# Token factors of the first block's residuals and norms: computed on columns, spread by TensorE between modulation slots

## Chip, core and metric

The kernel runs on one core of a Trainium2 chip. The metric is the device time of one execution in microseconds; lower is better. All arithmetic of the stages told of here is in 32-bit floats.

## What is computed

Two transformer blocks run one after the other on 256 tokens of width 1024. The first block (two layers) carries 256 context tokens along; its residual stream X therefore has 512 tokens until the middle of the second layer. Every norm in it has a gain and a shift that come from a small conditioning network (a vector times a 1024 x 6144 matrix for each layer):

```
rmsnorm(x, g) = x * rsqrt(mean(x*x) + EPS) * g
modulate(x, shift, scale) = x * (1 + scale) + shift
```

A layer does this twice, once with a mixer and once with a feed-forward part f:

```
y = f(modulate(rmsnorm(x, g0), shift, scale))
x = x + gate * rmsnorm(y, g1)
```

So each half of a layer has a norm in front of f and a residual behind it, and both need one factor for each token: 1 / sqrt(mean square + EPS).

## The kernel before

All activations lie with features on partitions: X is eight chunks of 128 features, each 128 partitions x n tokens (n is 512 or 256). The sum over features is therefore a sum over partitions, and TensorE makes it with a stationary matrix of ones: the result, wk[:, 0, 0:n], holds each token's sum on all 128 partitions at once. ScalarE takes the root of 128 x n values, VectorE the reciprocal of 128 x n values, and the factor multiplies each chunk.

The pieces, by their line numbers in the profile:

- A residual r (0 to 3): ScalarE squares each chunk of the branch's output Y as it arrives (L975), GpSimd adds them up in sq_acc (L982, L985). pe_residual makes one matmul for the sum (L990); act_residual takes the root (L995), with a table load ahead of it; dve_residual the reciprocal (L1001), and then for each chunk nt = Y times the factor (L1013) and X += gain times nt (L1007).
- A norm j (1 to 3): ScalarE squares each updated chunk of X (L743), pe_norm accumulates the sum chunk by chunk (L730), then root (L747) and reciprocal (L765), nt = X times the factor (L777), scaled and shifted by ScalarE (L757, "n" in the profile), rounded to the high part (L760), and the low part on VectorE (L772). The next projection takes high and low parts chunk by chunk.
- Residual 0 is followed by norm 1, residual 1 by norm 2 (both pairs on 512 tokens), residual 2 by norm 3 (256 tokens), residual 3 (256 tokens) by the second block's first norm, which the diff doesn't touch. Norm 0 isn't touched either.
- The conditioning matrices are worked off in modulation slots of 1 MB, spread over the first block wherever TensorE has room. A slot is eight matmuls (16 passes) of 256 columns in a quarter of the array each (L570, pe_ada_products), a staging copy by ScalarE (L580), and four passes with two moving columns that turn the previous slot's result onto partitions (L593, pe_ada_columns). Its weights lie in a ring of two buffers (ada_ring). ScalarE asks for the load of slot s + 2 only when it has staged slot s (L583).

The engines' programs are written out by hand, and each runs in its own order. In the pair residual 0 and norm 1, TensorE has nine slots (0 to 8 of the stage): 0 and 1, the residual's matmul, 2 and 3, then the norm's chunks with slots 4, 5, 6 behind chunks 1, 3 and 5, then 7 and 8. ScalarE stages 0 and 1, takes the root, stages 2 and 3, squares the norm's chunks with 4, 5 and 6 staged behind chunks 3, 5 and 7, takes the root, stages 7 and 8 (the `meanwhile` of act_norm), and only then scales. The pair residual 1 and norm 2 has the same order. A 32-bit matmul is two passes in the profile, each with its own weight load.

Of the kernel before, what the change touches and what calls it, by code (L numbers as in the profile page):

```python
# [20 lines left out]
ALU = mybir.AluOpType  # L21
# [3 lines left out]
P = 128  # L25
D = 1024
# [145 lines left out]
def stack_kernel(nc, t, out, layers):  # L172
# [3 lines left out]
    with ctx:  # L176
# [45 lines left out]
        sq = at("sq", [P, 2, T1], nt0 + 2 * KB)  # L222
        root = at("root", [P, T1], nt0 + 6 * KB)
        rstd = at("rstd", [P, T1], nt0 + 8 * KB)
        nt = at("nt", [P, 2, T1], nt0 + 10 * KB)
        n32 = at("n32", [P, 2, T1], nt0 + 14 * KB)

# [265 lines left out]
        def V(name, i=0, n=1):  # L493
            return vec[:, VEC[name] + i:VEC[name] + i + n]
# [228 lines left out]
        def squares_of(j):  # L723
            return (sq4, None, root4) if j == 4 else (sq2, sq2_acc, root2)

        def pe_norm(pe, j, between=None):
            n = NORMS[j][0]
            for c in range(DC):
                pe.wait_ge(nsq_ready, DC * j + c + 1)
                pe.matmul(wk[:, 0, 0:n], ones[:, :], sq[:, c % 2, 0:n], start=c == 0, stop=c == DC - 1)\  # L730
                    .then_inc(nsq_used, 1)
                if between:
                    between(c)

        def act_norm(act, j, meanwhile=None, between=None):
            n, x0, groups, gain, shift = NORMS[j]
            if j == 0:
                act.wait_ge(s_vec, 16)
            for c in range(DC):
                x_ready_for(act, j, c)  # L740
                if c >= 2:
                    act.wait_ge(nsq_used, DC * j + c - 1)
                act.activation(sq[:, c % 2, 0:n], X[:, c, x0:x0 + n], ACT.Square).then_inc(nsq_ready, 1)  # L743
                if between:
                    between(c)
            act.wait_ge(nsq_used, DC * (j + 1))
            act.activation(root[:, 0:n], wk[:, 0, 0:n], ACT.Sqrt, bias=V("eps"), scale=1.0 / D).then_inc(root_ready, 1)  # L747
            if meanwhile:
                meanwhile()
            act.wait_ge(s_gain, (4, 6, 8, 9)[j])  # L750
            for c in range(DC):
                act.wait_ge(nt_ready, DC * j + c + 1)
                if c >= 2:
                    act.wait_ge(h_ready, DC * j + c - 1)
                for i, (s, a, b) in enumerate(groups):
                    kw = {} if shift is None else {"bias": shift(s, c)}
                    ins = act.activation(n32[:, c % 2, a:b], nt[:, c % 2, a:b], ACT.Identity, scale=gain(s, c), **kw)  # L757
                ins.then_inc(n32_ready, 1)
                act.wait_ge(n32_ready, DC * j + c + 1)
                act.activation(H_hi[n][:, c, 0:n], n32[:, c % 2, 0:n], ACT.Copy).then_inc(hhi_ready, 1)  # L760

        def dve_norm(dve, j, meanwhile=None):
            n, x0, groups, gain, shift = NORMS[j]
            dve.wait_ge(root_ready, j + 1)
            dve.reciprocal(rstd[:, 0:n], root[:, 0:n]).then_inc(rstd_ready, 1)  # L765
            if meanwhile:
                meanwhile()
            dve.wait_ge(rstd_ready, j + 1)

            def lo(c):  # L770
                dve.wait_ge(hhi_ready, DC * j + c + 1)
                dve.tensor_tensor(H_lo[n][:, c, 0:n], n32[:, c % 2, 0:n], H_hi[n][:, c, 0:n].bitcast(F32),  # L772
                                  ALU.subtract).then_inc(h_ready, 1)
            for c in range(DC):
                if c >= 2:
                    dve.wait_ge(n32_ready, DC * j + c - 1)
                dve.tensor_tensor(nt[:, c % 2, 0:n], X[:, c, x0:x0 + n], rstd[:, 0:n], ALU.mult).then_inc(nt_ready, 1)  # L777
                if c >= 1:
                    lo(c - 1)
            lo(DC - 1)  # L780
# [56 lines left out]

        def dve_rstd(dve, j):
            n = WIDTH[j]
            dve.wait_ge(root_ready, j + 1)  # L840
            dve.reciprocal(rstd2[:, 0:n], squares_of(j)[2][:, 0:n]).then_inc(rstd_ready, 1)
            dve.wait_ge(rstd_ready, j + 1)

        BY_POOL = (3, 7)

        def final_norm(eng, by_pool):
            eng.wait_ge(rstd_ready, FINAL + 1)
# [90 lines left out]
        yroot_ready, yrstd_ready, yt_ready = sem("y_root_ready"), sem("y_rstd_ready"), sem("y_scaled_ready")  # L938

        def dve_y(dve, name, add=None, tail=None):  # L940

# [42 lines left out]
                    pool.wait_ge(ysq_used, DC * r + m)  # L984
                    pool.tensor_tensor(sq_acc[:, 0:n], sq_acc[:, 0:n], sq[:, m % 2, 0:n], ALU.add).then_inc(ysq_used, 1)  # L985

        def pe_residual(pe, r):
            n = RES[r][0]
            pe.wait_ge(ysq_used, DC * (r + 1))
            pe.matmul(wk[:, 1, 0:n], ones[:, :], sq_acc[:, 0:n], start=True, stop=True).then_inc(ysum_ready, 1)  # L990

        def act_residual(act, r):
            n = RES[r][0]
            act.wait_ge(ysum_ready, r + 1)
            act.activation(root[:, 0:n], wk[:, 1, 0:n], ACT.Sqrt, bias=V("eps"), scale=1.0 / D).then_inc(yroot_ready, 1)  # L995

        def dve_residual(dve, r):
            n, x0, groups, (layer, j), _ = RES[r]
            dve.wait_ge(s_gain, (5, 7, 8, 9)[r])
            dve.wait_ge(yroot_ready, r + 1)  # L1000
            dve.reciprocal(rstd[:, 0:n], root[:, 0:n]).then_inc(yrstd_ready, 1)  # L1001
            dve.wait_ge(yrstd_ready, r + 1)

            def update(c):
                dve.wait_ge(yt_ready, DC * r + c + 1)
                for s, a, b in groups:
                    ins = dve.scalar_tensor_tensor(X[:, c, x0 + a:x0 + b], nt[:, c % 2, a:b], gains[:, layer, j, s, c:c + 1],  # L1007
                                                   X[:, c, x0 + a:x0 + b], ALU.mult, ALU.add)
                ins.then_inc(x_ready, 1)
            for c in range(DC):  # L1010
                if c >= 2:
                    dve.wait_ge(x_ready, DC * r + c - 1)
                dve.tensor_tensor(nt[:, c % 2, 0:n], Y[:, c, 0:n], rstd[:, 0:n], ALU.mult).then_inc(yt_ready, 1)  # L1013
# [1719 lines left out]
        def pe_ffn_halves(pe, layer, j):  # L2733
            def slots(s):
                if ADA_FFN + s < ADA_LATE:
                    pe_ada(pe, ADA_FFN + s)
                elif ADA_FFN + s == ADA_LATE:
                    pe_ada_close(pe, ADA_LATE)
            pe_ffn(pe, layer, 0, j, slots if layer == 0 else None)
            pe_ffn(pe, layer, 1, j)  # L2740
            if layer == 0:
                for g in (0, 1):
                    pe_ada(pe, ADA_LATE + g)
            pe_residual(pe, j)
            if layer == 0:
                for g in (2, 3):
                    pe_ada(pe, ADA_LATE + g)

# [133 lines left out]
        def _(pe):  # L2882
# [14 lines left out]
                    ks=(0, 1, 2, 4, 5, 6, 7, 3), fill=lambda s, j: pe_hyb_out(pe, s, j))  # L2897
            for g in (0, 1):
                pe_ada(pe, ADA_OUT + g)
            pe_residual(pe, 0)  # L2900
            for g in (2, 3):
                pe_ada(pe, ADA_OUT + g)
            pe_norm(pe, 1, between=lambda c: pe_ada(pe, ADA_OUT + 4 + c // 2) if c in (1, 3, 5) else None)
            for g in (7, 8):
                pe_ada(pe, ADA_OUT + g)
            pe_ffn_halves(pe, 0, 1)
            pe_norm(pe, 2, between=lambda c: pe_ada(pe, ADA_LATE + 4 + c // 2) if c in (1, 3, 5) else None)
            for g in (7, 8):
                pe_ada(pe, ADA_LATE + g)
# [176 lines left out]
```

## Time and profile before

| what | us |
|---|---|
| median of 3 runs | 2080.07 |
| lowest and highest run | 2079.8, 2082.15 |
| profiled execution, its own time | 2080.6 |
| its span in the trace | 2078.9 |
| TensorE busy in the span | 1969.3 |
| VectorE busy | 1249.3 |
| ScalarE busy | 939.3 |

The span runs from the first to the last instruction; the profiled execution's own time is 1.7 us longer. TensorE's clock has two levels, 2.4 GHz (shown as 1.00) and 1.2 GHz (0.50); over the whole span the mean granted clock is 0.977.

### The profile page before, as it was taken

To read this page: it belongs to the slowest core of one execution; us is meant where nothing else is said; L and a number is where in the kernel's file an instruction comes from. 1 tells how busy PE (TensorE), PEld (TensorE's weight loads), DVE (VectorE), ACT (ScalarE), POOL (GpSimd) and SP (SyncE) were. 2 spreads that over 40 slices of the span, in tenths; PEclk is the share of its full clock that TensorE was granted. 3 is DMA by queue.
4 is the path that set the end of the run, shared out by engine and by line. 5 is a ranking of instruction groups with operands and counts; after the bars stand their busy time and mean duration, and the time that the engine had idled before them with its cause. 6 is when DMAs were issued, how large, how long until landed. Compare 5 with 4: busy or idle time off the path is not lost.

```text
span 2078.9 us, 33997 instructions
## 1 busy us (share of the span) xinstructions
PE 1969.3 (95%) x13365; PEld 1745.7 (84%) x13365; DVE 1249.3 (60%) x1809; ACT 939.3 (45%) x1464; POOL 288.3 (14%) x245
## 2 busy tenths in 40 slices
PE   5999989999999899999979998999999999989998
PEld 3776747778888489989969997998899999879997
DVE  6355355543654545667567676656975566787564
ACT  4344445322332332258466455346654444565353
POOL 2000113430542000021024140000010010000001
PEclk9999989999999899999989999999999999989999
DMA  8621464433223523222434544542344544324553
GB/s 356 214 78 61 162 223 154 171 115 118 83 87 104 182 101 123 82 81 82 145 126 157 186 162 138 183 149 82 134 159 173 181 166 143 110 87 168 183 182 122
DMA packets 43950, 296.77 MB, mean 143 GB/s; under 512 B 4976, under 2 KB 6128, under 8 KB 11696
## 3 DMA queue, kind: packets, MB, share of 16 engines
q1 hardware_dynamic: 36576, 247.48, 34.5%
q10 hardware_dynamic: 6048, 42.49, 5.9%
q0 software_dynamic: 1200, 5.02, 0.6%
q8 instruction: 91, 1.49, 0.3%
q14 instruction: 35, 0.29, 0.0%
HBM read 293.93 MB, written 1.05 MB: 142 GB/s over the span
## 4 chain that ended last, share of the span: by engine, by line
PE 83%; DVE 7%; ACT 4%; DMA 2%; issue 2%; POOL 1%; SPq 0%; ACTq 0%; DVEq 0%; POOLq 0%
PE acc L456 23%; PE acc L458 22%; PE acc L457 22%; DVE w_lo L393 2%; PE acc L451 2%; PE wk L570 2%; PE acc L452 2%; PE acc L453 2%; PE wk L1599 1%; DMA ada_first<-in_w_ada 1%; PE wk L730 1%; ACT w_hi L383 1%; PE wk L593 1%; DMA ada_ring<-in_w_ada 1%; PE wk L1329 1%
## 5 line engine op out<-in xcount | busy, mean ns | idle before, releaser
L456 PE MATMUL acc<-Hhi,w_hi 128*128 128x272 f32 (+2 forms) x2304 | 745.5, 324 | 31.1 <-DVE Hlo L772 9.1
L458 PE MATMUL acc<-Hhi,w_lo 128*128 128x272 f32 (+2 forms) x2304 | 721.9, 313 | 0.0
L457 PE MATMUL acc<-Hlo,w_hi 128*128 128x272 f32 (+2 forms) x2304 | 721.2, 313 | 0.0
L393 DVE TENSOR_TENSOR w_lo<-w_raw,w_hi 128x1024 fp32r<-128x1024 f32 (+2 forms) x472 | 586.8, 1282 | 201.1 <-ACT w_hi L383 199.5
L383 ACT ACTIVATE w_hi<-w_raw 128x1024 fp32r<-128x1024 f32 (+2 forms) x472 | 452.6, 1005 | 436.0 <-PE acc L458 356.7
L456 PEld LDWEIGHTS acc<-Hhi,w_hi 128*128 128x128 f32 x2304 | 441.9, 192 | 77.1 <-issue 36.6
L457 PEld LDWEIGHTS acc<-Hlo,w_hi 128*128 128x128 f32 x2304 | 442.3, 192 | 21.7
L458 PEld LDWEIGHTS acc<-Hhi,w_lo 128*128 128x128 f32 x2304 | 441.7, 192 | 22.5
L456 PE MATMUL acc<-Fhi,w_hi 128*128 128x256 f32 (+2 forms) x864 | 264.7, 306 | 5.1 <-POOL Flo L1086 5.1
L458 PE MATMUL acc<-Fhi,w_lo 128*128 128x256 f32 (+2 forms) x864 | 264.4, 306 | 0.0
L457 PE MATMUL acc<-Flo,w_hi 128*128 128x256 f32 (+2 forms) x864 | 264.1, 306 | 0.0
L456 PEld LDWEIGHTS acc<-Fhi,w_hi 128*128 128x128 f32 x864 | 163.4, 189 | 13.5 <-POOL Flo L1086 6.4
L458 PEld LDWEIGHTS acc<-Fhi,w_lo 128*128 128x128 f32 x864 | 163.5, 189 | 7.0
L457 PEld LDWEIGHTS acc<-Flo,w_hi 128*128 128x128 f32 x864 | 163.1, 189 | 6.6
L1042 ACT ACTIVATE cgu<-acc,vec 128x512 f32<-128x512 f32 (+1 forms) x88 | 58.2, 667 | 149.7 <-PE acc L458 149.5
L1064 DVE SCALAR_TENSOR_TENSOR cgu<-acc,vec,cgu 128x510 f32<-128x510 f32 (+1 forms) x88 | 52.1, 609 | 96.9 <-ACT cgu L1042 96.9
L451 PE MATMUL acc<-w_hi,Hhi 128*128 128x256 f32 x320 | 93.2, 291 | 0.0
L1083 POOL TENSOR_TENSOR hid<-sg,cgu 128x512 f32<-128x512 f32 (+1 forms) x44 | 44.8, 1018 | 335.4 <-ACT sg L1046 335.4
L452 PE MATMUL acc<-w_lo,Hhi 128*128 128x256 f32 x320 | 90.4, 283 | 0.0
L453 PE MATMUL acc<-w_hi,Hlo 128*128 128x256 f32 x320 | 90.4, 283 | 0.0
L813 POOL TENSOR_TENSOR sq_acc<-sq 128x272 f32<-128x272 f32 (+1 forms) x4 | 4.8, 1204 | 526.2 <-ACT sq L796 376.6
L1086 POOL TENSOR_TENSOR Flo<-hid,Fhi 128x256 f32 (+3 forms) x44 | 71.9, 1635 | 7.4 <-POOL Fhi L1084 7.0
(381 smaller groups left out, 2432.8 us busy)
## 6 DMA issues: line engine op xcount, KB each, us to landing
w_raw<-in_w_ffn_in SPq DMA_DIRECT2D x44, 1024.0 KB, 4.9
ada_ring<-in_w_ada ACTq DMA_DIRECT2D x40, 1024.0 KB, 4.9
w_raw<-in_w_mlp_in SPq DMA_DIRECT2D x32, 1024.0 KB, 4.8
w_raw<-in_w_mlp_out SPq DMA_DIRECT2D x32, 1024.0 KB, 4.9
w_raw<-in_w_ffn_out SPq DMA_DIRECT2D x32, 704.0 KB, 4.0
ada_first<-in_w_ada SPq DMA_DIRECT2D x8, 1024.0 KB, 18.1
w_raw<-in_w_ret_v SPq DMA_DIRECT2D x8, 1024.0 KB, 4.7
w_raw<-in_w_ret_g SPq DMA_DIRECT2D x8, 1024.0 KB, 4.8
```

Of the source, the lines that this page charges most:

```text
L383: act.activation(w_hi[:, r, a:b], w_raw[:, r, a:b], ACT.Copy).then_inc(hi_done, 1)
L393: dve.tensor_tensor(w_lo[:, r, a:b], w_raw[:, r, a:b], w_hi[:, r, a:b].bitcast(F32), ALU.subtract).then_inc(lo_done, 1)
L451: pe.matmul(o, x_hi(k)[:, toks], w_hi[:, r, w], start=k == 0, stop=False)
L452: pe.matmul(o, x_hi(k)[:, toks], w_lo[:, r, w], start=False, stop=False)
L453: mm = pe.matmul(o, x_lo(k)[:, toks], w_hi[:, r, w], start=False, stop=k == last)
L456: pe.matmul(o, w_hi[:, r, w], x_hi(k), start=k == 0, stop=False)
L457: pe.matmul(o, w_hi[:, r, w], x_lo(k), start=False, stop=False)
L458: mm = pe.matmul(o, w_lo[:, r, w], x_hi(k), start=False, stop=k == last)
L1042: act.activation(cgu[:, r, c, 0:n], acc_tile(p, r, c), ACT.Identity, bias=Vd("conv_b", m + layer * 44), scale=Vd("conv_w", m + (layer * 3 ...
L1064: dve.scalar_tensor_tensor(seqs(o, 1, SEQ), seqs(acc_tile(p, r, c), 0, SEQ - 1), w, seqs(o, 1, SEQ), ALU.mult, ALU.add).then_inc(conv_left, 1)
L1083: pool.tensor_tensor(hid[:, r, 0:n], left(r), right(r), ALU.mult).then_inc(hid_mul, 1)
L1086: pool.tensor_tensor(lo, hid[:, r, 0:n], hi.bitcast(F32), ALU.subtract).then_inc(hid_done, 1)
```

## The change

In the four residuals and in norms 1, 2 and 3 the square sums are made with tokens on partitions: for each tile of 128 tokens the squares are the stationary operand and one column of ones moves, so that the result is one column of 128 sums. Root and reciprocal then work on 128 x n/128 values (rcol). To bring the factor back to all partitions, VectorE scales the identity by it, one 128 x 128 diagonal for each tile, and TensorE multiplies ones by that diagonal (dve_spread, pe_spread); the factor is then read from PSUM (wk) by the scaling. pe_norm puts its sums into acc instead of wk.

TensorE's order changes: slot 2 now lies between a residual's sum and its spread, slot 3 behind the spread; in norms 1 and 2 slot 7 moves into the chunk loop, behind chunk 7, then comes the spread, then slot 8. ScalarE's order of slots stays. Semaphores of residuals and norms are merged (nth, spread_base).

The diff without its one-line renumberings of waits:

```diff
+        diag, rcol = root, at("rcol", [P, 8], nt0 + 8 * KB)
...
+        def pe_spread(pe, j, residual):
+            n, base = NORMS[j][0] if not residual else RES[j - 1][0], spread_base(j, residual)
+            for t in range(n // P):
+                pe.wait_ge(s_diag, base + t + 1)
+                pe.matmul(wk[:, 1 if residual else 0, t * P:(t + 1) * P], ones[:, :], diag[:, t * P:(t + 1) * P], start=True, stop=True)\
+                    .then_inc(s_spread, 1)
+
+        def dve_spread(dve, n, base):
+            for t in range(n // P):
+                dve.tensor_scalar(diag[:, t * P:(t + 1) * P], ident[:, :], rcol[:, 4 + t:5 + t], None, ALU.mult).then_inc(s_diag, 1)
+            dve.wait_ge(s_spread, base + n // P)
+
         def pe_norm(pe, j, between=None):
             n = NORMS[j][0]
             for c in range(DC):
                 pe.wait_ge(nsq_ready, DC * j + c + 1)
-                pe.matmul(wk[:, 0, 0:n], ones[:, :], sq[:, c % 2, 0:n], start=c == 0, stop=c == DC - 1)\
-                    .then_inc(nsq_used, 1)
+                for t in range(n // P):
+                    mm = pe.matmul(acc[:, t, 0:1], sq[:, c % 2, t * P:(t + 1) * P], ones[:, 0:1], start=c == 0, stop=c == DC - 1)
+                mm.then_inc(nsq_used, 1)
                 if between:
                     between(c)
+            pe_spread(pe, j, False)
...
-            act.activation(root[:, 0:n], wk[:, 0, 0:n], ACT.Sqrt, bias=V("eps"), scale=1.0 / D).then_inc(root_ready, 1)
+            act.activation(rcol[:, 0:n // P], acc[:, 0:n // P, 0:1].rearrange("p t s -> p (t s)"), ACT.Sqrt, bias=V("eps"), scale=1.0 / D)\
+                .then_inc(root_ready, 1)
...
-            dve.reciprocal(rstd[:, 0:n], root[:, 0:n]).then_inc(rstd_ready, 1)
+            dve.reciprocal(rcol[:, 4:4 + n // P], rcol[:, 0:n // P]).then_inc(rstd_ready, 1)
...
-                dve.tensor_tensor(nt[:, c % 2, 0:n], X[:, c, x0:x0 + n], rstd[:, 0:n], ALU.mult).then_inc(nt_ready, 1)
+                dve.tensor_tensor(nt[:, c % 2, 0:n], X[:, c, x0:x0 + n], wk[:, 0, 0:n], ALU.mult).then_inc(nt_ready, 1)
...
-        def pe_residual(pe, r):
+        def pe_residual(pe, r, between=None):
             n = RES[r][0]
             pe.wait_ge(ysq_used, DC * (r + 1))
-            pe.matmul(wk[:, 1, 0:n], ones[:, :], sq_acc[:, 0:n], start=True, stop=True).then_inc(ysum_ready, 1)
+            for t in range(n // P):
+                mm = pe.matmul(wk[:, 1, t:t + 1], sq_acc[:, t * P:(t + 1) * P], ones[:, 0:1], start=True, stop=True)
+            mm.then_inc(ysum_ready, 1)
+            if between:
+                between()
+            pe_spread(pe, r + 1, True)
...
-            pe_residual(pe, 0)
-            for g in (2, 3):
-                pe_ada(pe, ADA_OUT + g)
-            pe_norm(pe, 1, between=lambda c: pe_ada(pe, ADA_OUT + 4 + c // 2) if c in (1, 3, 5) else None)
-            for g in (7, 8):
-                pe_ada(pe, ADA_OUT + g)
+            pe_residual(pe, 0, between=lambda: pe_ada(pe, ADA_OUT + 2))
+            pe_ada(pe, ADA_OUT + 3)
+            pe_norm(pe, 1, between=lambda c: pe_ada(pe, ADA_OUT + 4 + c // 2) if c % 2 else None)
+            pe_ada(pe, ADA_OUT + 8)
```

The other lines that the diff replaces: residuals take the root and the reciprocal on rcol in the same way, with wk[:, 1, ...] as their PSUM row, and residual 1 and norm 2 get the new order of slots too.

## Rows read from the trace of the kernel before

**Rows 1.** Timeline of the first residual: start us, length us, engine, line, operation.

```profile
275.83 1.28 ACT L995 ACT_TABLE_LOAD   x1
277.13 0.69 ACT L995 ACTIVATE root<-wk,vec 128x512 f32<-128x512 f32 x1
...
277.56 1.07 PE L570 MATMUL wk<-ada_ring,cvec 128*32 128x256 f32 x16 [0.84 <-DMA ada_ring<-in_w_ada]
277.92 3.35 DVE L1001 RECIPROCAL rstd<-root 128x512 f32<-128x512 f32 x1 [5.42 <-ACT root L995]
...
278.56 0.61 PE L593 MATMUL wk<-vec,ada_rows 128*128 128x2 f32 x4
...
281.30 1.29 DVE L1013 TENSOR_TENSOR nt<-Y,rstd 128x512 f32<-128x512 f32 x2
```

**Rows 2.** Chain of waits in norm 1: start us, length us, what was waited for.

```profile
284.11 3.78 PE wk L730 x4
287.88 1.36 PE wk L570 x16
289.25 0.54 PE wk L593 x4
289.79 1.82 PE wk L730 x4
...
296.62 4.81 DMA ada_ring<-in_w_ada
...
304.20 1.10 ACT n L757 x2
```

**Rows 3.** Chain of waits around norm 2, the same columns.

```profile
691.63 7.06 DMA ada_ring<-in_w_ada
698.73 1.93 PE wk L570 x16
700.66 0.96 PE wk L593 x4
...
706.57 1.86 PE wk L570 x16
...
722.95 1.09 ACT n L757 x2
```

**Rows 4.** Groups by shape: count, busy us, mean ns, idle before.

```profile
L1452 DVE TENSOR_SCALAR s_sb<-s_sb,tiny 128x256 f32<-128x256 f32 x16 | 4.9, 351 | 0.3
...
L1251 DVE TENSOR_TENSOR g_sb<-wk,sgu_b 128x512 f32<-128x512 f32 x4 | 2.8, 692 | 9.0 <-PE wk L1184 9.0
...
L1448 DVE RECIPROCAL tiny<-tiny 128x2 f32<-128x2 f32 x16 | 2.6, 162 | 8.2 <-ACT s_sb L1369 8.2
...
L1214 ACT ACTIVATE tiny<-tiny,vec 128x4 f32<-128x4 f32 x1 | 0.3, 297 | 0.0
```

**Rows 5.** Weight loads of L593, two stretches: length, busy (count), granted clock, DMA.

```profile
22.92:24.04 1.12, 1.04 (x8) 1.00 0.97 402
700.50:701.70 1.20, 0.93 (x4) 0.50 0.00 0
```

**Rows 6.** TensorE in four stretches, then L593 alone in two of them.

```profile
278.60:281.80 3.20, 1.78 (x26) 1.00 0.79 259
281.80:284.10 2.30, 0.66 (x4) 0.50 1.00 328
284.10:288.60 4.50, 4.49 (x12) 0.50 0.53 215
...
691.30:694.90 3.60, 1.91 (x20) 1.00 1.01 410
...
691.30:694.90 3.60, 0.21 (x2) 1.00 1.01 410
...
278.60:281.80 3.20, 0.78 (x6) 1.00 0.79 259
```

**Rows 7.** Chain of waits in the third residual (256 tokens).

```profile
1047.85 1.76 DVE rstd L1001
```

More of the change, by code:

```diff
@@ L724, in squares_of, with nth, spread_base @@
             return (sq4, None, root4) if j == 4 else (sq2, sq2_acc, root2)
+        s_diag, s_spread = sem("token_factor_diagonal"), sem("token_factor_spread")
+        def nth(j):
+            return 2 * j + 1 if j < 4 else j + 5
+        def spread_base(j, residual):
+            e = 2 * (j - 1) + (0 if residual else 1)
+            return 4 * min(e, 4) + 2 * max(e - 4, 0)
+        def pe_spread(pe, j, residual):
[8 more added lines that the diff above has]
+            dve.wait_ge(s_spread, base + n // P)
         def pe_norm(pe, j, between=None):
@@ L760, in act_norm, with dve_norm @@
                 act.activation(H_hi[n][:, c, 0:n], n32[:, c % 2, 0:n], ACT.Copy).then_inc(hhi_ready, 1)
-        def dve_norm(dve, j, meanwhile=None):
+        def dve_norm(dve, j):
             n, x0, groups, gain, shift = NORMS[j]
-            dve.wait_ge(root_ready, j + 1)
-            dve.reciprocal(rstd[:, 0:n], root[:, 0:n]).then_inc(rstd_ready, 1)
-            if meanwhile:
-                meanwhile()
-            dve.wait_ge(rstd_ready, j + 1)
+            dve.wait_ge(root_ready, nth(j))
+            dve.reciprocal(rcol[:, 4:4 + n // P], rcol[:, 0:n // P]).then_inc(rstd_ready, 1)
+            dve.wait_ge(rstd_ready, nth(j))
+            dve_spread(dve, n, spread_base(j, False))
             def lo(c):
@@ L839, in dve_rstd @@
             n = WIDTH[j]
-            dve.wait_ge(root_ready, j + 1)
+            dve.wait_ge(root_ready, nth(j))
             dve.reciprocal(rstd2[:, 0:n], squares_of(j)[2][:, 0:n]).then_inc(rstd_ready, 1)
-            dve.wait_ge(rstd_ready, j + 1)
+            dve.wait_ge(rstd_ready, nth(j))
         BY_POOL = (3, 7)
         def final_norm(eng, by_pool):
-            eng.wait_ge(rstd_ready, FINAL + 1)
+            eng.wait_ge(rstd_ready, nth(FINAL))
             for c in range(DC):
@@ L937, in stack_kernel @@
         ysq_ready, ysq_used, ysum_ready = sem("y_square_ready"), sem("y_square_added"), sem("y_sum_ready")
-        yroot_ready, yrstd_ready, yt_ready = sem("y_root_ready"), sem("y_rstd_ready"), sem("y_scaled_ready")
+        yt_ready = sem("y_scaled_ready")
         def dve_y(dve, name, add=None, tail=None):
@@ L994, in act_residual @@
             act.wait_ge(ysum_ready, r + 1)
-            act.activation(root[:, 0:n], wk[:, 1, 0:n], ACT.Sqrt, bias=V("eps"), scale=1.0 / D).then_inc(yroot_ready, 1)
+            act.activation(rcol[:, 0:n // P], wk[:, 1, 0:n // P], ACT.Sqrt, bias=V("eps"), scale=1.0 / D).then_inc(root_ready, 1)
         def dve_residual(dve, r):
@@ L999, in dve_residual @@
             dve.wait_ge(s_gain, (5, 7, 8, 9)[r])
-            dve.wait_ge(yroot_ready, r + 1)
-            dve.reciprocal(rstd[:, 0:n], root[:, 0:n]).then_inc(yrstd_ready, 1)
-            dve.wait_ge(yrstd_ready, r + 1)
+            dve.wait_ge(root_ready, 2 * r + 2)
+            dve.reciprocal(rcol[:, 4:4 + n // P], rcol[:, 0:n // P]).then_inc(rstd_ready, 1)
+            dve.wait_ge(rstd_ready, 2 * r + 2)
+            dve_spread(dve, n, spread_base(r + 1, True))
             def update(c):
@@ L1012, in dve_residual @@
                     dve.wait_ge(x_ready, DC * r + c - 1)
-                dve.tensor_tensor(nt[:, c % 2, 0:n], Y[:, c, 0:n], rstd[:, 0:n], ALU.mult).then_inc(yt_ready, 1)
+                dve.tensor_tensor(nt[:, c % 2, 0:n], Y[:, c, 0:n], wk[:, 1, 0:n], ALU.mult).then_inc(yt_ready, 1)
                 if c >= 1:
@@ L2743, in pe_ffn_halves @@
                     pe_ada(pe, ADA_LATE + g)
-            pe_residual(pe, j)
+            pe_residual(pe, j, between=(lambda: pe_ada(pe, ADA_LATE + 2)) if layer == 0 else None)
             if layer == 0:
-                for g in (2, 3):
-                    pe_ada(pe, ADA_LATE + g)
+                pe_ada(pe, ADA_LATE + 3)
         def store_out(sp):
@@ L2899, in _ @@
                 pe_ada(pe, ADA_OUT + g)
-            pe_residual(pe, 0)
-            for g in (2, 3):
-                pe_ada(pe, ADA_OUT + g)
-            pe_norm(pe, 1, between=lambda c: pe_ada(pe, ADA_OUT + 4 + c // 2) if c in (1, 3, 5) else None)
-            for g in (7, 8):
-                pe_ada(pe, ADA_OUT + g)
+            pe_residual(pe, 0, between=lambda: pe_ada(pe, ADA_OUT + 2))
+            pe_ada(pe, ADA_OUT + 3)
+            pe_norm(pe, 1, between=lambda c: pe_ada(pe, ADA_OUT + 4 + c // 2) if c % 2 else None)
+            pe_ada(pe, ADA_OUT + 8)
             pe_ffn_halves(pe, 0, 1)
-            pe_norm(pe, 2, between=lambda c: pe_ada(pe, ADA_LATE + 4 + c // 2) if c in (1, 3, 5) else None)
-            for g in (7, 8):
-                pe_ada(pe, ADA_LATE + g)
+            pe_norm(pe, 2, between=lambda c: pe_ada(pe, ADA_LATE + 4 + c // 2) if c % 2 else None)
+            pe_ada(pe, ADA_LATE + 8)
             pe_ada_close(pe, ADA_RING)
```

## Prediction

> **What bounds the kernel now.** I read the page first: TensorE is busy for 1969.3 of 2078.9 us (the table above), so almost everywhere time is matmul time. The exceptions are the stages that the diff touches. There I read the timeline of the first 512-token residual, the chain of waits through the norm behind it, then the same chain in the second pair, and at last the stretches with their granted clock.
>
> In the residual [rows 1] the reader is to see a short serial chain. The square root starts at 277.13, behind the table load and not behind TensorE; the reciprocal takes 3.35 us over 512 columns; the scaling starts at 281.30. TensorE meanwhile has modulation slot 2 of the stage (277.56, wide products of 1.07 us) and its columns (278.56, 0.61 us).
>
> In the norm [rows 2] the chain is on TensorE: a pair of chunks costs 1.82 us, a slot 1.0 + 0.54 us. Slot 4 starts at T = 287.88; the scaled outputs start at 304.20, T + 16.3. What ends last in front of them isn't the reciprocal but slot 8, whose weights were requested at 296.62 and needed 4.81 us. In the second pair the distance is the same, 722.95 - 706.57 = 16.4 [rows 3]. So behind both norms a queue of modulation slots (two buffers, the next load issued only when a slot has been staged) ends last, and a faster reciprocal there releases nothing.
>
> **The change part by part.**
>
> *Root and reciprocal on columns.* The 512-wide root and reciprocal (0.69 + 3.35 us) become a 128x4 activation, nearest row 0.30 us, and a 128x4 reciprocal, nearest row 0.16 us for 128x2 [rows 1, 4]. Four 128x128 scalings by a pointer are added; the 128x256 row takes 0.35 us and the 512 row 0.48, so I extrapolate 0.285 us each and, with the overlap that pairs show (two scalings of 0.69 in 1.29), 0.22 us start to start: 0.95 for four, 0.5 for two. The scaling that follows reads its factor from PSUM; a 128x512 operation with one PSUM operand took 0.69, as long as now: nothing [rows 4].
>
> *First residual.* The root would end at 277.43, the four diagonals at about 278.8. But the spreading matmuls stand on TensorE behind slot 2 and its columns, which end at 279.10. Eight passes at 0.135 us and 0.2 to drain give 280.35 against 281.30: a gain of 0.95, not the 2 that the vector side offers. The spread is queued ahead of slot 3, which then starts at 280.3 at the earliest; before, its load and not TensorE set its start, as slot 2's did (0.84 us idle in its row). The sum itself (one 512-column matmul before, four one-column ones now) stays under the table load.
>
> *Chunks of the norm.* One matmul with 512 moving columns, stationary ones, becomes four with one moving column and the squares stationary: eight weight loads for two. The nearest rows are the two-column passes that close a slot [rows 5]: eight in 1.12 us at the full clock (0.14 each), and at the low clock four loads in 0.93 us, each 0.34 long, so (0.93 - 0.34)/3 = 0.20 each. A chunk then costs 1.11 us against 0.91 at 2.4 GHz, and 1.6 against 1.89 (3.78 for two) at 1.2 GHz [rows 2, 5]. The Trainium skill, "TensorE: Matmul & The Clock Gate", section "LDWEIGHTS (loading the stationary operand)", says that a load's time goes by its columns, 0.107 us for 128, whatever the rows. By it a chunk would be 0.85 us, 0.26 less than by the row, and with the clock kept the norms would lose nothing. The row shows 1.12, and the row goes into the sum.
>
> *The clock.* This decides. Here the rows are stretches with TensorE's granted clock [rows 6]. From 278.6 to 281.8 TensorE was busy 1.78 us, 0.78 of it in two-column passes; the clock stood at 0.50 from 281.8 on. From 691.3 to 694.9 it was busy 1.91 us, but only 0.21 of that in two-column passes, and no such fall came behind it. I read this as: narrow passes don't hold the clock as wide ones do. From 284.1 to 288.6 it was busy without a gap, all wide, and the clock still stood at 0.50. In the changed norm the wide work in a pair is one slot's products, 1.0 us of 3.75 at the full clock: a smaller share than the 1.0 us of 3.2 behind which it fell. I therefore take it that the clock falls (or stays low, as the first chunks are low already) through both 512-token norms. At 1.2 GHz a slot takes 1.93 + 0.96 = 2.89 us [rows 3], a pair 3.2 + 2.89 = 6.1.
>
> *Norms 1 and 2, low clock.* From T: three pairs 18.3; slot 7, now inside, 2.9; the spread 1.9 (eight passes of 128 columns, each a quarter of the 0.945 us that a 512-column pass took there [rows 2]); slot 8, 2.9, now behind the spread; its staging 0.45. Sum 26.4 against 16.3: +10.0 each. The root and the diagonals lie under slot 7 and cost nothing; without that cover they would be 1.7 us. ScalarE waits for slot 8 before its first scaled output, as before; VectorE's second halves and the next projection wait for that. T itself comes earlier. In norm 1 the squares arrive 0.95 sooner and two chunks at 1.6 save 0.5: -1.45. In norm 2 the squares start behind slot 3's columns (700.66 + 0.96), and its weights took 7.06 us [rows 3], so the residual's gain is lost there and only the chunks' 0.55 is left. Norm 1: +8.55. Norm 2: +9.45.
>
> *The 256-token stages* (residuals 2 and 3, norm 3). No slots stand here. The reciprocal (1.76 us, [rows 7]) and a root of about 0.5 (an estimate between 0.69 and 0.30 [rows 1, 4]) become 0.3 + 0.2 + 0.5 + 0.5: -0.8 for each residual, rounded up a little since the last diagonal hides part of the first matmul. In norm 3 chunks are 4 x 0.20 = 0.8 us at the low clock, no longer than before (two 256-column passes of half 0.945 each), and the spread at the low clock takes 0.3 more: -0.5. Sum -2.1.
>
> *Total:* 8.55 + 9.45 - 2.1 = +15.9 us. The profiled execution took 2080.6 us around a span of 2078.9, and the median of the runs is 2080.07; I add to the median: 2096.0.
>
> *Bounds of the unknown prices.* Low-clock pass: 0.17 us (two of four loads at either clock) to 0.24 (passes with their tail): -3 to +5 us over both norms. The phase in which the clock rises in the projection behind each norm: 3 us either way in all. Diagonals 0.2 to 0.35 each: below 1 us. That the clock holds is a case of its own.
>
> **The rivals.**
>
> *The clock holds (other side).* One mechanism: back-to-back narrow passes keep TensorE busy enough, and it rises in the second pair of chunks as now. For it: TensorE is never idle there, and eight narrow passes at 22.9 us ran at 1.00 between wide ones [rows 5]. Against it: the stretches from 278.6 and 691.3 [rows 6]. Then a pair costs 2.2 + 1.54 = 3.75 against 3.36, but slot 8 waits on the ring of buffers anyway: slot 6 at T + 7.5, slot 8 another 1.0 + 0.54 + 0.2 for staging + 4.81 = 6.6 later, outputs 2.7 behind it at T + 16.8, +0.4 for each norm. Sum -1.45 - 0.55 + 0.8 - 2.1 = -3.3: 2076.8. It decides as soon as the pairs of chunks run at 2.4 GHz. The same page of the Trainium skill, section "What's actually happening", states that the clock follows how busy the array has been, without a word on moving columns; taken plainly it speaks for this rival, and no run here shows it yet.
>
> *Only one norm is slow,* or the clock comes back in the middle (the spread and slot 8 are wide and adjacent): about half, +8: 2088.
>
> *The slots don't hold the end,* because their loads come early and the full 4.04 us less 2.1 is won at four sites: -7.7 - 2.1 = -9.8: 2070. Against it: slot 8's load is the last thing before the outputs in both norms [rows 2, 3].
>
> *The spread is stuck behind a late slot.* Slot 2 or 7 stands ahead of it in TensorE's queue; a load of 7.06 us as at 691.63 instead of 4.81 delays the spread by 2.2 us at one or two of four places, with the clock kept: -3.3 + 2 to 4, no change: 2080.
>
> **How the numbers follow.** Low clock in both norms 0.66, own range 2089 to 2103; clock holds 0.16 (2075 to 2079); one norm or half 0.08; full gain 0.04; stuck spread 0.06. A change within 0.2% (4.2 us) is about what a measurement of this kernel can't tell from none. Faster: the full gain 0.04 and 0.06 of the holding clock, 0.10. Same: 0.10 of it and 0.03 of the stuck spread, 0.13. Slower: 0.77. The range 2076 to 2102 leaves out the full gain and the outer parts of the first two cases, together under 0.2.
>
> **What would show it.** The granted clock between slot 4 and the scaled outputs in both norms: 0.5 if I am right, about 1.0 if the first rival is. The distance from slot 4's products to the first scaled output: 26 against 16.8. Chunk passes 0.14 or 0.20 us apart. Scaling in the first residual at 280.35, and 0.8 us earlier in the 256-token ones. I am wrong if one-column passes keep the clock, or if loads with the squares stationary are cheaper than the columns of a slot.

## Result and the profile after

| | before | after |
|---|---|---|
| median us | 2079.94 (2079.34 to 2082.15, 4 runs) | 2096.99 (2096.26 to 2098.99, 4 runs) |
| ratio | 1 | 1.0081, 95% interval 1.0068 to 1.0094 |
| span of the profiled execution | 2078.9 | 2095.0 |
| mean granted clock | 0.977 | 0.967 |

The changed kernel is 0.8% slower: 17.0 us between the medians, 16.1 between the spans.

Where it arises is read from the same event in both traces. The chain of waits of the changed kernel through the first residual and norm 1 (start us, length us, what was waited for; L571 is a slot's products, L594 its columns, L740 the spread, L753 the norm's one-column sums, L782 the scaled outputs):

```profile
277.24 1.93 PE wk L571 x16
279.17 0.94 PE wk L594 x4
280.11 1.92 PE wk L740 x8
282.03 1.87 PE wk L571 x16
...
285.61 2.14 PE acc L753 x16
287.75 1.86 PE wk L571 x16
289.61 0.94 PE wk L594 x4
290.55 3.41 PE acc L753 x16
...
309.21 1.91 PE wk L740 x8
...
314.49 1.10 ACT n L782 x2
```

It answers to [rows 1, 2]. The reader is to see four things. The scaling of the first residual waits behind slot 2 (1.93 + 0.94) and the spread (1.92 for eight passes): it starts at 282.07, 0.8 us later than before and not earlier. Slot 4 starts at 287.75, where it did before (287.88). From there to slot 8 every piece is at its slow length: 1.86 for a slot's products, 3.41 for sixteen one-column passes, that is 0.213 us each. And inside the norm no DMA stands in the chain any more: where before slot 8's load of 4.81 us ended last, TensorE itself does now. The scaled outputs start at 314.49 against 304.20: +10.3.

TensorE in five stretches of the same kernel (stretch, length, busy and count, granted clock, DMA share, GB/s), and behind them one of the kernel before:

```profile
275.00:284.00 9.00, 8.07 (x57) 0.62 0.83 294
284.00:300.00 16.00, 14.82 (x92) 0.60 0.52 177
300.00:304.00 4.00, 4.00 (x27) 0.50 0.25 104
698.00:702.00 4.00, 3.19 (x44) 1.00 0.90 340
706.00:718.00 12.00, 10.82 (x73) 0.64 0.54 178
...
284.00:300.00 16.00, 15.77 (x96) 0.86 0.67 239
```

From 284 to 304 the engine is idle for 1.2 us and runs at 0.60 and then 0.50; before, it stood at 0.86 from 284 to 300. At the end of the projection between the two norms it is at the full clock (698 to 702), and norm 2 shows the same fall. Its chain:

```profile
706.48 1.91 PE wk L740 x8
708.39 1.87 PE wk L571 x16
...
712.10 1.97 PE acc L753 x16
714.06 1.86 PE wk L571 x16
...
716.87 3.41 PE acc L753 x16
...
740.64 1.09 ACT n L782 x2
```

Slot 4 of this pair starts at 714.06 (before 706.57), the outputs at 740.64 (before 722.95, [rows 3]): +17.7.

In the 256-token residual the forecast pieces are there (timeline of the third residual; L1015 the sum, L1024 the root, L1030 the reciprocal, L745 the diagonals, L1043 the scaling):

```profile
1065.97 0.61 PE L1015 MATMUL wk<-ones,sq_acc 128*128 128x1 f32 x4 [1.77 <-POOL sq_acc L1009]
1066.61 0.26 ACT L1024 ACTIVATE rcol<-wk,vec 128x2 f32<-128x2 f32 x1 [1.50 <-PE wk L1015]
1066.97 0.17 DVE L1030 RECIPROCAL rcol<-rcol 128x2 f32<-128x2 f32 x1 [2.31 <-ACT rcol L1024]
1067.18 0.48 DVE L745 TENSOR_SCALAR root<-ident,rcol 128x128 f32<-128x128 f32 x2
...
1067.52 0.71 PE L740 MATMUL wk<-root,ones 128*128 128x128 f32 x4 [0.94 <-DVE root L745]
1068.27 0.42 DVE L1043 TENSOR_TENSOR nt<-Y,wk 128x256 f32<-128x256 f32 x1 [0.61 <-PE wk L740]
```

From the sum to the scaling it takes 2.30 us. Before, sum, root and reciprocal took 3.1, of which 1.76 was the reciprocal [rows 7]. The offset against before (how much later the same event comes) falls by 0.80 here and by 0.80 again in the fourth residual.

The offset of the changed kernel, event by event:

| event | offset us |
|---|---|
| scaling, residual 0 | +0.8 |
| outputs, norm 1 | +10.3 |
| outputs, norm 2 | +17.7 |
| sum, residual 2 | +19.4 |
| outputs, norm 3 | +18.6 |
| scaling, residual 3 | +18.3 |
| end of the span | +16.1 |

So norms 1 and 2 make all of it. Two larger steps lie outside the changed stages: +1.8 in the retention stage (near 910 us) and -2.5 in the second block (near 1860 us, from +18.6 to +16.1). Both lie in stretches in which both kernels have an episode of lower clock, and the two kernels have it at other places and lengths: around 1850 to 1880 the clock stood at 0.66, 0.78, 0.88 in three stretches of 10 us before, and at 0.83 in one such stretch after.

### The profile page after: what moved, and what is told of

The parts are those of the page before. It is cut to its first block, busy times and chain, and to the rows that moved or that the text cites. A ratio compares the mean times of both kernels' runs of the same rounds, so it can differ in the third digit from the quotient of the medians.

```text
span 2095.0 us, 34363 instructions
## 1 busy us (share of the span) xinstructions
PE 1996.4 (95%) x13537; PEld 1781.9 (85%) x13537; DVE 1238.3 (59%) x1831; ACT 938.0 (45%) x1464; POOL 287.6 (14%) x245
## 3 DMA queue, kind: packets, MB, share of 16 engines
HBM read 293.93 MB, written 1.05 MB: 141 GB/s over the span
## 4 chain that ended last, share of the span: by engine, by line
PE 84%; DVE 7%; ACT 4%; DMA 2%; issue 1%; POOL 1%; SPq 0%; ACTq 0%; DVEq 0%; POOLq 0%
PE acc L457 22%; PE acc L459 22%; PE acc L458 21%; PE wk L571 2%; DVE w_lo L394 2%; PE acc L452 2%; PE acc L453 2%; PE acc L454 2%; PE acc L753 2%; PE wk L1629 1%; DMA ada_first<-in_w_ada 1%; PE wk L594 1%; ACT w_hi L384 1%; PE wk L1359 1%; PE acc L1618 1%
## 6 DMA issues: line engine op xcount, KB each, us to landing
ada_first<-in_w_ada SPq DMA_DIRECT2D x8, 1024.0 KB, 18.3
```

## Experiments

What each run gave, with the granted clock in three stretches and the start of the first scaled output of norms 1, 2 and 3. The column "sums" gives the moving columns of residuals / norms ("wide" is as before, ones stationary and all tokens moving). Clock and outputs are those of one profiled execution each; the medians are of 4 to 11 runs.

| kernel | sums | median us | ratio, 95% interval | clock 275-284, 284-300, 706-718 | outputs us |
|---|---|---|---|---|---|
| before | wide / wide | 2079.94 | | .88 .86 .90 | 304.2, 723.0, 1061.0 |
| after (the changed kernel) | 1 / 1 | 2096.99 | 1.0081, 1.0068 to 1.0094 | .62 .60 .64 | 314.5, 740.6, 1079.6 |
| e1 | 128 / 128 | 2074.32 | 0.9963, 0.9951 to 0.9975 | 1.00 1.00 1.00 | 302.2, 720.4, 1057.1 |
| e2 | 1 / wide | 2077.85 | 0.9992, 0.9982 to 1.0001 | .81 1.00 .90 | 302.3, 718.9, 1056.0 |
| e3 | wide / 1 | 2098.91 | 1.0092, 1.0077 to 1.0108 | .78 .50 .50 | 313.8, 740.8, 1078.8 |
| e4 | wide / wide, short root | 2079.99 | 0.9996, 0.9987 to 1.0006 | .90 .85 .88 | 304.5, 722.8, 1061.0 |
| e5 | 64 / 64 | 2096.69 | 1.0076, 1.0060 to 1.0091 | 1.00 .55 .64 | 312.7, 739.2, 1080.2 |
| e6 | 32 / 32 | 2098.89 | 1.0088, 1.0072 to 1.0103 | .70 .50 .64 | 315.8, 742.3, 1083.3 |
| e7 | 128 / 128, old order of slots | 2078.05 | 0.9990, 0.9981 to 0.9999 | .62 .79 1.00 | 308.9, 725.5, 1062.4 |
| e8 | 1 / 128 | 2075.66 | 0.9981, 0.9972 to 0.9991 | .59 .80 1.00 | 307.9, 722.6, 1059.3 |
| e9 | 1 / 1 and a filler of 256 | 2112.44 | 1.0162, 1.0144 to 1.0179 | .68 .50 .72 | 320.1, 747.1, 1093.2 |
| e10 | 128 / wide | 2075.37 | 0.9976, 0.9965 to 0.9986 | .81 1.00 .93 | 303.7, 719.7, 1056.9 |
| e11 | 1 / 1 and a filler of 512 | 2118.72 | 1.0187, 1.0170 to 1.0204 | .68 .61 .72 | 319.2, 759.8, 1104.5 |
| e12 | 128 / 1 and a filler of 512 | 2109.97 | 1.0156, 1.0138 to 1.0174 | .81 .58 .94 | 321.3, 747.7, 1092.7 |

Each ratio is against runs of the kernel before on the same chip (medians 2080.62 for e1 to e4, 2080.11 for e5 to e8, 2080.64 for e9 and e10, 2079.6 for e11 and e12).

### Same order, same passes, 128 columns moving (e1)

```diff
-                    mm = pe.matmul(acc[:, t, 0:1], sq[:, c % 2, t * P:(t + 1) * P], ones[:, 0:1], start=c == 0, stop=c == DC - 1)
+                    mm = pe.matmul(acc[:, t, 0:128], sq[:, c % 2, t * P:(t + 1) * P], ones[:, 0:128], start=c == 0, stop=c == DC - 1)
...
-                mm = pe.matmul(wk[:, 1, t:t + 1], sq_acc[:, t * P:(t + 1) * P], ones[:, 0:1], start=True, stop=True)
+                mm = pe.matmul(wk[:, 1, t * P:t * P + 128], sq_acc[:, t * P:(t + 1) * P], ones[:, 0:128], start=True, stop=True)
```

> The changed kernel with one difference: the square sums of norms 1 to 3 and of the residuals move 128 columns of ones instead of one. The number of passes and of weight loads stays, and each pass should still be as long as its load (0.14 us at 2.4 GHz against 128 columns in two passes of 0.11), so at a given clock nothing is gained. My theory (one-column passes don't hold the clock): the clock rises behind the first chunks of both norms as in the kernel before, the distance from slot 4 to the scaled outputs falls from 26.8 to about 17, and the time to 2075 to 2080, as far below the changed kernel as my sum put the low clock above (about 18 us). Rival (the number of narrow passes and the longer queue cost the time, the low clock follows from that, and the columns don't matter): 2097 or a little more, clock 0.50 through the norms as now.

This is the deciding run. It has the changed kernel's instructions, number for number; only the square sums move 128 columns for one. It takes 22.7 us less than the changed kernel (medians 2074.32 and 2096.99), 0.4% less than before. Its six runs lie between 2069.55 and 2076.35. Its chain:

```profile
279.68 1.01 PE wk L740 x8
...
280.72 1.28 DVE nt L1044 x2
...
286.18 1.00 PE wk L571 x16
...
287.72 1.89 PE acc L753 x16
...
294.69 5.25 DMA ada_ring<-in_w_ada
...
302.15 1.10 ACT n L782 x2
```

and its stretches:

```profile
275.00:284.00 9.00, 6.65 (x72) 1.00 0.92 330
284.00:300.00 16.00, 14.67 (x153) 1.00 0.78 268
...
706.00:718.00 12.00, 11.60 (x119) 1.00 0.78 264
```

The scaling of residual 0 starts at 280.7, near the forecast 280.35. Sixteen passes take 1.89 us, 0.118 each, against 3.41 for one moving column. Slot 8's load of 5.25 us ends last again, as before, and the outputs start 16.0 us behind slot 4 (16.4 in norm 2). So it is the clock that costs, and in the norms the width of the moving side decides whether it is granted.

### Which half of the change (e2, e3, e10)

e2 takes only the residuals' part of the diff, e3 only the norms', e10 is e2 with 128 columns moving in the residuals' sums. The core of e2 against the changed kernel:

```diff
-                for t in range(n // P):
-                    mm = pe.matmul(acc[:, t, 0:1], sq[:, c % 2, t * P:(t + 1) * P], ones[:, 0:1], start=c == 0, stop=c == DC - 1)
-                mm.then_inc(nsq_used, 1)
+                pe.matmul(wk[:, 0, 0:n], ones[:, :], sq[:, c % 2, 0:n], start=c == 0, stop=c == DC - 1)\
+                    .then_inc(nsq_used, 1)
...
-            pe_spread(pe, j, False)
```

> Only the four residuals on columns, with slot 2 ahead of their spread; norms 1 to 3 as in the kernel before. Theory: norms keep their wide passes and the clock, so the 17 us go. Residual 0 and 1 give nothing or cost a little (the clock fell during the narrow sum at 277 and the first scaling came 0.8 us late), residuals 2 and 3 give 0.8 each: 2077 to 2082. Rival (residuals carry half of the loss): about 2088.

> Only norms 1 to 3 on columns, with slot 7 ahead of their spread; the residuals as in the kernel before. Theory: both 512-token norms run at 1.2 GHz from the end of their first chunks on, +10 us each from slot 4 to the scaled outputs, less 0.5 for each in the first two chunks: 2096 to 2100. Rival (half and half): about 2088. Where residual and norm are only slow together, because the clock falls in the residual's narrow sum: about 2082.

> Residuals on columns with 128 moving columns, norms as in the kernel before. Against the run with 128 columns everywhere (2074.3) it tells what the norms' own columns earn. By the queue of slots: nothing at the 512-token norms, 0.7 at norm 3, so 2074 to 2076. If the norms' cheap factor counts: 2077 to 2080.

e3 has all of the loss: clock 0.50 through both norms, outputs at 313.8 and 740.8 as in the changed kernel. e2 and e10 have none of it: the outputs start 1.9 and 0.5 us earlier than before in norm 1, 4.1 and 3.3 in norm 2, 5.0 and 4.1 in norm 3. By its median e10 is faster than before (interval below 1); e2 can't be told from before. e1 and e10 overlap in their intervals, so putting the norms' sums on columns as well is worth nothing that these runs can show.

### The root and reciprocal of the norms (e4)

The kernel before, with root and reciprocal of norms 1 and 2 over 4 of 512 values; the factor of the other tokens is left out.

```diff
-            act.activation(root[:, 0:n], wk[:, 0, 0:n], ACT.Sqrt, bias=V("eps"), scale=1.0 / D).then_inc(root_ready, 1)
+            k = n if j == 3 else 4
+            act.activation(root[:, 0:k], wk[:, 0, 0:k], ACT.Sqrt, bias=V("eps"), scale=1.0 / D).then_inc(root_ready, 1)
...
-            dve.reciprocal(rstd[:, 0:n], root[:, 0:n]).then_inc(rstd_ready, 1)
+            dve.reciprocal(rstd[:, 0:k], root[:, 0:k]).then_inc(rstd_ready, 1)
```

> The kernel before with root and reciprocal of norms 1 and 2 made over 4 columns instead of 512, so that most tokens of these norms are scaled by an older factor (that part of the computation is left out). It gives the whole gain of a cheap factor and nothing of the change's costs. Theory (the queue of modulation slots ends last in front of the scaled outputs): the first scaled output starts at most 0.3 us earlier in each norm, the time is 2079 to 2080. Rival (the reciprocal ends last): 3 us and more earlier in each, 2073 to 2074.

The outputs start at 304.5 and 722.8 against 304.2 and 723.0, and the ratio is 0.9996: the 512-wide reciprocals of norms 1 and 2 were free. What the change wanted to save there was not on the path.

That holds for the kernel before. In norm 1 of e2 the same reciprocal stands in the chain, and no load of a slot behind it:

```profile
297.63 3.36 DVE rstd L786
```

### How many moving columns (e5, e6)

As e1 with 64 and 32 in place of 128 in both edits.

> As the run with 128 moving columns, but 64. The passes are as many and as long (their loads set the length), so only what the array streams in each is halved. If the clock follows the moving columns, the clock in both norms stands somewhere between the two cases: it either holds and the time is that of 128 columns (2074), or stays low and the time is that of one column (2097), or one norm of each: 2085. If anything wider than one column were enough, 2074.

> The same with 32 moving columns. By the theory of moving columns it lies nearer to the changed kernel than 64 does: the clock at 0.50 through both norms and 2092 to 2098. By the rival (any width above one is enough) 2074.

Neither helps: 2096.69 and 2098.89, like one column, with the outputs at 312.7 and 315.8. TensorE in two stretches of the kernel with 64 columns:

```profile
275.00:284.00 9.00, 6.66 (x71) 1.00 0.94 335
284.00:300.00 16.00, 15.89 (x100) 0.55 0.50 188
```

It was busy for 15.89 of 16 us at 0.55. So busy time on the profile isn't what the clock follows here: before, 15.77 us busy had 0.86, and in e1 14.67 had 1.00. The run with 64 held 1.00 through the residual and into norm 1 (its first eight passes took 1.10 us at 284.48, the next sixteen, from 288.40, took 3.52), the one with 32 did not. The split is the same in every norm on 512 tokens: in the four kernels that move 1, 32 or 64 columns and have no filler (the changed one, e3, e5, e6), each further sixteen passes took 3.41 to 3.52 us, in norm 1 and in norm 2; in the three that move 128 (e1, e7, e8) they took 1.89 to 1.91. Only the first passes of a norm, ahead of slot 4, come at either clock in both groups. Widths between 64 and 128 weren't run.

### What the residual's narrow sum does (e8)

As e1, but the residuals' sums move one column.

> 128 moving columns in the norms, one column in the residuals' sums as in the changed kernel. In the profile of the changed kernel the clock fell at 277, during the first residual's narrow sum, and cost it 1.7 us against my sum (scaling at 282.07 instead of 280.35). If that fall comes from the narrow sum: 1.5 to 2 us above the run with 128 columns everywhere, 2076, with the clock low at 277. If it only depends on where the fall happens to lie: the same 2074.

The low clock is there (0.59 from 275 to 284), but it isn't the narrow sum that brought it. The eight one-column passes stand in the chain with 1.86 us, at the low clock from the first on:

```profile
276.73 1.86 PE wk L1015 x8
```

So the clock fell ahead of them. In the changed kernel, too, it didn't fall during this sum, as the expectation has it: the passes took 1.05 us from 275.53, at the full clock, and the clock fell at about 277, behind them. It fell at nearly the same place in kernels whose residuals move 128 columns: the eight passes of the sum took 2.09 us from 276.42 in e7, 2.07 from 276.01 in e10 and 2.08 from 276.35 in e12. Of the residuals' sums with 128 columns only e1's held 1.00 from 275 to 284. The width of this sum therefore doesn't decide the clock in the first residual; what does stays open.

Norm 1's outputs start at 307.9 against 302.2 in e1. Of these 5.8 us, 4.6 are there when slot 4 starts (290.75 against 286.18), and 1.2 are slot 8's load (6.48 us against 5.25). In norm 2 the difference is 2.2 us. The median, 2075.66, is near the 2076 given for a fall that comes from the narrow sum, but that condition isn't what the trace shows. It and e1's 2074.32 were measured apart, each against its own runs of before, and the intervals overlap (up to 0.9975 and from 0.9972): that the residual's sum alone costs anything in total isn't shown.

### The order of the slots (e7)

As e1, with TensorE's slots in the order of the kernel before: the spread stands ahead of slots 2 and 3, and in the norm ahead of 7 and 8.

```diff
-            pe_residual(pe, 0, between=lambda: pe_ada(pe, ADA_OUT + 2))
-            pe_ada(pe, ADA_OUT + 3)
+            pe_residual(pe, 0)
+            for g in (2, 3):
+                pe_ada(pe, ADA_OUT + g)
```

> 128 moving columns, but the modulation slots in the order of the kernel before: in the residuals the spread comes straight behind the sum and slots 2 and 3 behind it, in norms 1 and 2 the spread follows chunk 7 and slots 7 and 8 follow the spread. TensorE then waits for the diagonals with nothing to do, about 1.5 us at each of four places, but where the load of slot 8 (ring of two buffers) ends last that wait is free. If the ring is what ends last: within 1.5 us of the other order, either side (2073 to 2076). If the new order matters in itself: 2078 to 2080.

The outputs start at 308.9 and 725.5 against 302.2 and 720.4 in e1, and the median is 2078.05, 3.7 us above e1 with intervals apart. So with 128 columns this order is the slower one; why is shown only in part. In the chain of norm 1 the spread (303.39, 1.16 us) stands ahead of the products of slots 7 (304.55) and 8 (306.71), and only then come the outputs. But of the 6.7 us in norm 1, 4.9 are there when slot 4 starts (291.10 against 286.18), behind a residual in which the clock was low (0.62 from 275 to 284). The 5.1 us in norm 2 are mostly these 6.7 carried on and no second loss: slot 4 starts 3.2 us later there (707.15 against 703.95), and the rest is the load that ends last, 7.14 us against 5.07 in e1:

```profile
715.66 7.14 DMA ada_ring<-in_w_ada
```

It was issued behind slot 6 in both orders. What the order itself costs, apart from where the clock fell and how long that load took, these runs don't separate.

### Wide work between the narrow passes (e9, e11, e12)

The changed kernel with one more matmul behind each chunk's one-column matmuls; nobody reads its result. e9 moves 256 columns, e11 and e12 all tokens of the norm, and e12 also has the residuals' sums of e1.

```diff
+                mm = pe.matmul(wk[:, 0, 0:n], ones[:, :], sq[:, c % 2, 0:n], start=True, stop=True)
                 mm.then_inc(nsq_used, 1)
```

> The changed kernel with its one-column passes as they are, and behind the four of each chunk of norms 1 to 3 one more matmul with 256 moving columns whose result nobody reads: 24 matmuls of useless work. If the low clock is the loss: at 2.4 GHz the filler costs 0.43 us a chunk, a pair 2 x (1.11 + 0.43) + 1.54 = 4.6 us against 6.2 at 1.2 GHz, the distance from slot 4 to the scaled outputs about 19 to 20 instead of 26.7, and the time 2081 to 2086, 11 to 16 us below the changed kernel although it does more. If the narrow passes themselves are the loss and the clock only goes along: 24 x 0.43 to 24 x 0.85 on top, 2107 to 2117.

> Left out or changed: nothing of the result; in norms 1 to 3 each chunk's one-column matmuls are followed by one more matmul of the same squares with the full token width moving (512 columns in norms 1 and 2, 256 in norm 3), whose result nobody reads. It is twice as wide as in the run before, which did not bring the clock back. If wide columns in sufficient share hold the clock although the narrow passes stay: granted clock about 1.0 in norms 1 and 2, a pair of chunks with its slot 2 x (0.94 + 0.91) + 1.54 = 5.2 us, slot 4 to scaled outputs about 20 us (26.7 in the changed kernel, with less work), total about 2090 us, below the changed kernel. If the clock stays at 0.50 in spite of it: a pair 2 x (1.7 + 1.89) + 2.8 = 10 us, distance about 38 us, total about 2131 us. Up to the first pair of norm 1 the clock may be low in both, since the residual's sum stays narrow.

> As the filler of full width, and the residual's sum moves 128 columns of ones in place of one (the root reads the first of each 128), so that the clock does not fall ahead of norm 1. If the clock follows the wide share from stretch to stretch: as the filler alone, with the first pair of norm 1 at the full clock too, 3 to 6 us less than it; distance in both norms about 20 us, total 2085 to 2089 us. If one-column passes pull the clock down whatever stands between them: it falls within the first pairs of norm 1 and the distance is about 38 us, total about 2128 us.

I had expected the filler to bring the clock back, and that failed: all three are slower than the changed kernel. e9 (2112.4) lies in the 2107 to 2117 given for its rival, that the narrow passes are the loss and the clock only goes along. It doesn't show that rival, since the clock, which was to be held, was 0.50 from 284 to 300; there the fillers simply came on top. Late in both norms it came back all the same (eight passes in 0.89 us from 309.50 and from 732.41). e11 (2118.7) and e12 (2110.0) lie between their two numbers, since the clock is neither held nor simply low: in e11 it alternates in norm 1 and stays low through norm 2. In norm 2 of e12 it goes up and down once in each pair of chunks. The chain:

```profile
722.34 1.55 PE wk L571 x16
723.88 0.54 PE wk L594 x4
724.42 0.89 PE acc L753 x8
725.31 0.97 PE wk L754 x2
726.28 0.87 PE acc L753 x8
727.15 1.92 PE wk L754 x2
729.07 1.59 PE wk L571 x16
730.66 0.54 PE wk L594 x4
...
747.67 1.09 ACT n L783 x2
```

and TensorE's clock over some of these stretches:

```profile
724.00:726.00 2.00, 2.00 (x14) 1.00 0.30 41
726.00:728.00 2.00, 2.00 (x10) 0.71 0.84 348
728.00:730.00 2.00, 2.00 (x14) 0.50 0.32 135
730.00:732.00 2.00, 2.00 (x25) 0.94 0.00 0
732.00:734.00 2.00, 2.00 (x12) 0.92 0.89 258
734.00:736.00 2.00, 2.00 (x6) 0.50 0.67 274
```

Nothing waits here; TensorE is busy throughout. Eight one-column passes take 0.89 us at the full clock (0.111 each) and 1.71 at the low one (norm 1 of the same run, at 292.49; 0.214 each), a 512-column filler 0.97 or 1.92. The clock falls at the end of the second chunk's one-column passes: the filler behind them (727.15) takes 1.92. Ahead of the fall stand a slot's columns, a chunk, a filler and the second chunk, all at 1.00. It rises within the slot's products (729.07, 1.59 us, against 1.00 at the full and 1.86 at the low clock), ahead of which stand the filler and the wide products. Even with a filler behind every chunk it falls again in each pair. Why one filler in each chunk isn't enough, these runs don't say.

The run also weighs the price: from slot 4's products to the first output norm 2 takes 25.3 us in e12 (722.34 to 747.67) and 26.6 in the changed kernel, although e12 has six fillers more in that stretch. More work in less time, at a higher clock (0.64 and 0.82 from 718 to 740, against 0.50). In norm 1, where the clock came back only for the last pair, the same distance is 31.6 us (289.68 to 321.29) against 26.7.

## Why the prediction was right

Forecast 2096.0, measured 2096.99. By its steps:

- **The clock falls through norms 1 and 2** (chance 0.66): shown. e1 against the changed kernel shows it with nothing else altered, e3 that the norms are the place, e5 and e6 that 32 and 64 columns do no better. The reading of [rows 6] that led there, that the two-column passes made the fall at 281.8 in the kernel before, wasn't tested: no run changed them, and the stretch ahead of that fall also held 1.42 us of idle time. The conclusion came true; that this premise did isn't shown. The first rival (the clock holds, 2076.8) is what e1 does: 2074.3, distance 16.0 against the 16.8 given for it. The rule of the Trainium skill, "TensorE: Matmul & The Clock Gate", section "What's actually happening", that the clock follows how busy the array has been, holds here only if "busy" isn't the busy time of the profile: 15.89 of 16 us at 0.55 in e5.
- **Distance from slot 4 to the outputs, 26.4:** 26.7 and 26.6. Slots 2.89: 2.80 to 2.83. Pair 6.1: 6.2. The low-clock pass, taken as 0.20: 0.213.
- **Norm 1, +8.55:** measured +10.3. The step that went wrong is the first residual's gain of 0.95, which was summed at the full clock. The clock fell at about 277, ahead of slot 2. Slot 2, its columns and the spread then ran at the low clock, and the scaling came 0.8 us late. What made it fall there is open: the eight one-column passes of the residual's own sum (1.05 us) stand ahead of it, but e7, e10 and e12 fall at nearly the same place with 128 columns. Slot 3 and its staging then held up the first squares, so that the first chunk started 1.5 us later than before (285.61 against 284.11). Two chunks at 2.14 us instead of 3.78 gave that back, so T moved by -0.13 and not by -1.45.
- **Norm 2, +9.45:** measured +7.4 (10.3 to 17.7). Slot 2's load, which had taken 7.06 us, took 4.71, and the first two chunks ran at the full clock, 1.97 us instead of the 3.2 forecast. The two misses cancel, 17.7 against 18.0, and that is luck.
- **256-token residuals, -0.8 each:** -0.80 and -0.80. **Norm 3, -0.5:** -0.03. Eight chunks took 7.00 us against 6.8 before, and four spreading passes 1.23 at the low clock. From the last sum to the first output: 2.6 us against 2.8.
- **Root and diagonals:** 0.26 and 0.18 for root and reciprocal, 0.87 for four diagonals (forecast 0.30, 0.16, 0.95).
- **One-column chunk at the full clock, 1.11:** 0.89 (e12), as much as the 512-column matmul it replaces. That was mis-sized: the row that I took [rows 5] had the start and end of a slot's columns in it. By the Trainium skill's 0.107 us for 128 columns (the same page, "LDWEIGHTS (loading the stationary operand)") it would have been 0.85, and the 0.89 of this run agrees with it to 0.04. At the low clock a pass took twice as long, 0.213. So one of the prediction's own signs of being wrong, loads with the squares stationary that are cheaper than the columns of a slot, did come true at the full clock. It had little weight in the result, since all but the first two chunks of norms 1 and 2 ran at the low one.
- **The total:** 17.7 + (-0.8 - 0.03 - 0.8) is +16.1, which is what the spans give. On the way there are +1.8 near 910 us, +0.4 between norm 3 and the fourth residual and -2.2 behind it, in stretches that the diff doesn't touch, and they cancel, by luck again. The forecast's 15.9 within 0.2 of the spans is therefore better than its parts were. Why the low-clock episodes of those stages lie differently stays open; it wasn't tried.

The version to take is e1: 2074.3 us, 0.4% below before. e10 can't be told from it (the intervals overlap), with the smaller change.

## What to carry to other kernels

Turning a reduction so that the data are stationary and one column moves costs a weight load for each tile and leaves almost no columns moving, and the clock can halve for everything around it: 17 us here. Try a full tile of moving columns (here 128 kept the clock in the norms and 64 did not), even if 127 of the results are thrown away: it cost 0.007 us a pass. And before shortening an operation, look in the chain of waits for what ends last ahead of the consumer: in both norms it was the ring of modulation slots, and the 3.35 us reciprocal was free. Look again once something else has moved: in e2 the same reciprocal had come onto the path.

## What the hardware showed that I had not expected

- A pass with one moving column and one with 128 cost nearly the same at the full clock, 0.111 us (e12) and 0.118 (e1); in the norms the difference is whether the clock is granted.
- TensorE without a gap doesn't mean 2.4 GHz: 0.55 over 16 us with 15.89 busy (e5), 0.50 from 284 to 300 with 16.00 busy (e3).
- The clock can alternate within a steady load: once per pair of chunks, some 6.7 us, in norm 2 of e12, with slot, filler and narrow passes all repeated alike. In norm 2 of e11 the same passes ran at the low clock throughout.
- In the first residual the clock fell at 276 to 277 in some kernels with 1 and some with 128 moving columns in the sum (1: the changed one, e8; 128: e7, e10, e12), and later or not at all in others. What a single profile shows there isn't yet an effect of the edit.
- A 1 MB load of a slot took 4.71 us in one kernel and 7.06 at the same place in another. In norm 2 of e7 the load that ends last took 7.14 us against 5.07 in e1, and slot 4 to the outputs took 18.3 us against 16.4.
